# A two-product split matmul in one 512-column record: wide up projections and joined operands in a fused transformer kernel

## The reference, cut to what matters

```python
def sq_relu_mlp(h, w_in, w_out):            # both MLPs: 1024 -> 4096 -> 1024
    a = jax.nn.relu(h @ w_in)
    return (a * a) @ w_out

def conv_glu(h, w_up, conv_w, conv_b, w_down):   # 1024 -> 2 x 2816 -> 1024
    gate, val = jnp.split(h @ w_up, 2, axis=-1)
    gate = depthwise_conv(gate, conv_w, conv_b)  # three taps along the tokens
    return (jax.nn.silu(gate) * val) @ w_down
```

## Time and profile before

| | |
|---|---|
| median of 3 runs | 1146.64 us (1145.39 to 1147.46) |
| the profiled execution | 1149.56 us |
| its span in the trace | 1147.8 us |
| granted TensorE clock, mean | 0.968 |
| PE busy | 1036.6 us, 90% |
| DVE busy | 708.3 us, 62% |
| ACT busy | 551.6 us, 48% |

### The profile page before, as it was taken

The page is one execution under the profiler, slowest core; times in us unless marked ns, Lnnn a source line. Parts: engine busy times, 40 slices in busy tenths (PEclk is TensorE's granted clock), DMA queues, the critical chain, the costliest instruction groups (busy, mean ns, idle before and its releaser), DMA issues.

```text
span 1147.8 us, 15792 instructions
## 1 busy us (share of the span) xinstructions
PE 1036.6 (90%) x6172; PEld 897.9 (78%) x6172; DVE 708.3 (62%) x964; ACT 551.6 (48%) x746; POOL 97.3 (8%) x74
## 2 busy tenths in 40 slices
PE   3877899999999997889999999999789779999995
PEld 1655579888897876779999887989666568999994
DVE  5566655788766547466767664455477466666664
ACT  3464636676544556444545443542533235544442
POOL 0003000575300010000000000000000000000000
PEclk9897999999999999989999999999999889999998
DMA  4342436677753553455777642332200044544531
GB/s 170 103 123 107 129 111 237 252 275 261 293 183 110 183 183 110 147 184 210 278 293 276 224 186 74 111 124 97 97 15 0 1 165 148 205 178 176 208 128 55
DMA packets 28976, 183.92 MB, mean 160 GB/s; under 512 B 3456, under 2 KB 4992, under 8 KB 9344
## 3 DMA queue, kind: packets, MB, share of 16 engines
q1 hardware_dynamic: 23328, 153.69, 36.6%
q0 software_dynamic: 3456, 25.17, 6.1%
q10 hardware_dynamic: 2144, 4.42, 1.6%
HBM read 180.64 MB, written 2.62 MB: 160 GB/s over the span
## 4 chain that ended last, share of the span: by engine, by line
PE 54%; issue 20%; DVE 13%; ACT 7%; DMA 4%; POOL 1%; DVEq 0%; ACTq 0%; POOLq 0%; SPq 0%
PE bank L619 15%; PE bank L620 14%; PE bank L621 14%; DVE split L1656 4%; ACT split L1166 4%; PE bank L628 2%; DMA raw<-w_mlp 2%; PE bank L1075 1%; PE bank L1057 1%; PE bank L855 1%; DMA work<-in_ctx 1%; DVE acts L1824 1%; POOL stat L550 1%; ACT arena L1167 1%; DMA t5c<-in_t_cols 1%
## 5 line engine op out<-in xcount | busy, mean ns | idle before, releaser
L1656 DVE TENSOR_TENSOR split<-raw,split 128x2048 fp32r<-128x2048 f32 (+3 forms) x133 | 301.5, 2267 | 296.0 <-ACT split L1166 290.4
L1166 ACT ACTIVATE split<-raw 128x2048 fp32r<-128x2048 f32 (+3 forms) x133 | 247.5, 1862 | 307.3 <-PE bank L621 272.8
L619 PE MATMUL bank<-acts,split 128*128 128x256 f32 (+1 forms) x1024 | 290.6, 284 | 1.4 <-DVE split L1656 1.1
L620 PE MATMUL bank<-acts,split 128*128 128x256 f32 (+1 forms) x1024 | 289.7, 283 | 0.0
L621 PE MATMUL bank<-acts,split 128*128 128x256 f32 (+1 forms) x1024 | 289.6, 283 | 0.0
L619 PE MATMUL bank<-split,acts 128*128 128x512 f32 (+3 forms) x616 | 243.7, 396 | 32.8 <-DVE split L1656 9.7
L620 PE MATMUL bank<-split,acts 128*128 128x512 f32 (+3 forms) x616 | 238.9, 388 | 0.0
L621 PE MATMUL bank<-split,acts 128*128 128x512 f32 (+3 forms) x616 | 238.1, 386 | 0.0
L619 PEld LDWEIGHTS bank<-acts,split 128*128 128x128 f32 (+1 forms) x1024 | 194.8, 190 | 5.5 <-DVE split L1656 2.3
L620 PEld LDWEIGHTS bank<-acts,split 128*128 128x128 f32 (+1 forms) x1024 | 194.8, 190 | 2.2
L621 PEld LDWEIGHTS bank<-acts,split 128*128 128x128 f32 (+1 forms) x1024 | 194.7, 190 | 0.4
(11 more groups left out here) (233 smaller groups left out, 1113.5 us busy)
## 6 DMA issues: line engine op xcount, KB each, us to landing
raw<-w_mlp SPq DMA_DIRECT2D x64, 1024.0 KB, 4.9
raw<-w_glu SPq DMA_DIRECT2D x22, 1024.0 KB, 5.4
work<-w_ada POOLq DMA_DIRECT2D x12, 1024.0 KB, 5.1
raw<-w_qkv SPq DMA_DIRECT2D x12, 1024.0 KB, 4.8
bias<-w_ada POOLq DMA_DIRECT2D x12, 1024.0 KB, 5.1
arena<-w_glu_down SPq DMA_DIRECT2D x22, 512.0 KB, 3.3
raw<-w_mla_o SPq DMA_DIRECT2D x4, 1024.0 KB, 4.8
raw<-w_moba_o SPq DMA_DIRECT2D x4, 1024.0 KB, 4.8
```

Of the source, the lines that this page charges most:

```text
L619: pe.matmul(out_, a[0], b[0], start=first, stop=False)
L620: pe.matmul(out_, a[0], b[1], start=False, stop=False)
L1166: return act.activation(out_, in_, ACT.Copy)
L1656: v.tensor_tensor(split[:, c % 2, 1, 0:n], raw[:, c % 2, 0:n], split[:, c % 2, 0, 0:n].bitcast(F32), ALU.subtract).then_inc(lo_ready, 1)
```

## The change

A new record form, `wide_product`: the high part of the weights multiplies the high and the low part of the tokens in one 512-column matmul, the high part's result in columns 0 to 255 of a bank and the low part's in 256 to 511; the low part of the weights times the high part of the tokens is a 256-column matmul into columns 0 to 255. The two halves must be added by whoever empties the bank, and each 128 features take a whole bank, so an up step takes two banks.

- The first 14 of 16 up steps of each MLP (`WIDE = 14`) and all 22 of the GLU take this form: 32 records in place of 48. The last two of each MLP stay as they were.
- MLPs: DVE adds the halves with two `tensor_reduce` operations (`halves_added`) ahead of `split_lo` in its queue, into `relu_t`; ACT's relu then reads and writes `relu_t`.
- GLU: DVE adds the halves of gate and value with two `tensor_reduce` operations into `gsum`, first in its step; the middle tap waits for the first of them (`glu_gate`) and reads `gsum`, as do the outer taps and the product.
- dt, xs and B: `both_unit` has latents and context as the two halves of a 512-column moving operand, three records in place of six.

```diff
+            def wide_product(bank, w, f, k):
+                ws = tuple(p[:, k, f * P:(f + 1) * P] for p in w)
+                pe.matmul(bank[:, :].rearrange("p (a b) -> p a b", a=2), ws[0], acts[:, 0, :, k * T:(k + 1) * T],
+                          start=k == 0, stop=False)
+                return pe.matmul(bank[:, 0:T], ws[1], acts[:, 0, 0, k * T:(k + 1) * T], start=False, stop=k == KD - 1)
...
+                    elif s < WIDE:
+                        wide_unit(c0 + n, u0, s, i)
                     else:
-                        cols_unit(c0 + n, u0 + up_step(name, s), (0, 1), (0, 0), i)
+                        gemm_gone(pe, u0 + WIDE - 1)
+                        cols_unit(c0 + n, u0 + up_step(name, s), (0, 1), (0, 0))
...
+            def both_unit(c, u, f):
+                w = slot(c, KD, 256)
+                gemm_start(u)
+                for k in range(KD):
+                    ins = product(gbank(u)[:, :].rearrange("p (a b) -> p a b", a=2),
+                                  tuple(p[:, k, f * P:(f + 1) * P] for p in w), both_pair(k), k == 0, k == KD - 1)
+                ins.then_inc(gemm_ready, 1)
...
                 for f in range(2):
-                    cols_unit(GC["xs"] + j, GU["xs"] + 2 * j + f, (f, f), (0, 1))
+                    both_unit(GC["xs"] + j, GU["xs"] + 2 * j + f, f)
...
-                act.activation(gact[:, b, :], gbank(u)[:, 0:T], ACT.Identity, scale=w, bias=bb).then_inc(glu_mid, 1)
+                act.wait_ge(glu_gate, 4 * k + (s + 1))
+                act.activation(gact[:, b, :], gsum[:, b, 0:T], ACT.Identity, scale=w, bias=bb).then_inc(glu_mid, 1)
...
+                    for f, bank in enumerate(wide_banks(GU[name], s)):
+                        ins = v.tensor_reduce(relu_t[:, s % 2, f * T:(f + 1) * T],
+                                              bank[:, :].rearrange("p (a b) -> p b a", a=2), AX.X, ALU.add)
...
                 def chunk(n, i=None):
+                    if not seq[n][0] and seq[n][1] < WIDE:
+                        halves_added(seq[n][1], i)
                     used(c0 + n, i, 8)
...
+                gemm_out(v, u, i)
+                for f, bank in enumerate(wide_banks(GU["glu"], s)):
+                    v.tensor_reduce(gsum[:, b, f * T:(f + 1) * T], bank[:, :].rearrange("p (a b) -> p b a", a=2), AX.X,
+                                    ALU.add).then_inc(gemm_free[u % 4] if f else glu_gate, 1)
                 v.wait_ge(glu_mid, 4 * k + (s + 1))
```

More of the change, by code:

```diff
@@ L148 @@
 HID0 = dict(mlp0=0, mlp1=16, glu=32)
+WIDE = 14
+RELU0 = dict(mlp0=0, mlp1=WIDE)
 RAW = ("m0", "h1", "m1")
@@ L300, in program @@
         prod_t = view(arena, 2048, 2, T)
+        gsum = view(arena, 2560, 2, 2 * T)
         final = arena[:, 8192:8192 + D]
@@ L702, in cols_unit, with wide_start, wide_unit, first_wide @@
                 ins.then_inc(gemm_ready, 1)
+            def wide_start(u0, s, i=None):
+                if s < 2:
+                    gemm_start(u0 + 2 * s)
+                    gemm_start(u0 + 2 * s + 1)
+                else:
+                    u = u0 + s - 2
+                    pe.wait_ge(gemm_free[u % 4], u // 4 + 1 if i is None else i + (u // 4 + 1))
+            def wide_product(bank, w, f, k):
[3 more added lines that the diff above has]
+                return pe.matmul(bank[:, 0:T], ws[1], acts[:, 0, 0, k * T:(k + 1) * T], start=False, stop=k == KD - 1)
+            def wide_unit(c, u0, s, i=None):
+                w = slot(c, KD, 256)
+                wide_start(u0, s, i)
+                for f, bank in enumerate(wide_banks(u0, s)):
+                    for k in range(KD):
+                        ins = wide_product(bank, w, f, k)
+                ins.then_inc(gemm_ready, 1)
+            def first_wide(c, u0, name, tiles=4, units=2):
+                w = slot(c, KD, 256)
+                wide_start(u0, 0)
+                for k0 in range(0, KD, tiles):
+                    pe.wait_ge(act_lo, LO[name] - 4 + units * (k0 // tiles + 1))
+                    for f, bank in enumerate(wide_banks(u0, 0)):
+                        for k in range(k0, k0 + tiles):
+                            ins = wide_product(bank, w, f, k)
+                ins.then_inc(gemm_ready, 1)
             def first_up(c, u, name, tiles=4, units=2):
@@ L894, in modulation_and_context @@
                     pe.wait_ge(normed, 4)
+                    gemm_gone(pe, GU["mlp1"] + WIDE - 1)
                     for m in range(4):
@@ L926, in _, with both_pair @@
             values(1, 0)
+            def both_pair(k):
+                return tuple(acts[:, :, p, k * T:(k + 1) * T] for p in range(2))
+            def both_unit(c, u, f):
+                w = slot(c, KD, 256)
+                gemm_start(u)
+                for k in range(KD):
+                    ins = product(gbank(u)[:, :].rearrange("p (a b) -> p a b", a=2),
+                                  tuple(p[:, k, f * P:(f + 1) * P] for p in w), both_pair(k), k == 0, k == KD - 1)
+                ins.then_inc(gemm_ready, 1)
             both = rows_of(0) + rows_of(1)
@@ L932, in _ @@
             w = slot(c, KD, 16)
[L933 to L936, removed]
+            for k in range(KD):
+                ins = product(gbank(u)[0:16, :].rearrange("p (a b) -> p a b", a=2), tuple(p[:, k, :] for p in w),
+                              both_pair(k), k == 0, k == KD - 1)
             ins.then_inc(gemm_ready, 1)
```

47 lines of the change are left out of this document (33 added, 14 removed).

## The result

The changed kernel took 1152.72 us (median of 6 runs, 1151.77 to 1158.68) against 1146.76 for the kernel before (6 runs, 1145.39 to 1150.11): ratio 1.0063, 95% interval 1.0041 to 1.0086, some 6 us slower. The forecast was 1144.9 and its range ended at 1151.5. The profiled execution took 1151.77 us, span 1149.9, so in the traces only 2.1 of the 6 us are to be seen. The rest is looked for in the granted clocks of all runs, at the end of the part on the prediction.

A forecast was written before the change was run, and what follows sets the result against it. PE was taken to bound the joined stage, the GLU's steps and most of `mlp1`, with splits or ACT/DVE chains elsewhere. Joined −2.2, `mlp0` −2.0, `mlp1` −1.3 and GLU +3.8 gave −1.7 on 1146.64: 1144.9 us, range 1139.5 to 1151.5.

The forecast's parts named there:

- What bounds the kernel: PE sets the pace in some stretches, splits or ACT/DVE chains in others; the GLU chain's 0.33 us slack decides.
- The cost of a record: Each PE record has a fixed cost of 0.0133 us, so wide pairs save 0.21 us per up step.
- Rival (b): Two-piece operands pay the fixed cost twice, so PE gains nothing: total +7.4, 1154.0 us; chance 0.10.
- Joined: In dt, xs and B, 56 tiles save 0.040 us each, all of it passing: −2.2 us.
- `mlp0`: Shorter ups in the first MLP, about half hidden between down 3 and down 10: −2.0 us.
- Rival (c): Reductions are slow, by their own rate or beside POOL in `mlp0`: total +4 to +8, around 1152; chance 0.12.
- `mlp1`: In the second MLP, +1.3 before the first down, then twelve wide steps at PE's pace, −2.56: sum −1.3 us.
- The +1.3: At `mlp1`'s start two reductions stand before `split_lo`, so the first down comes 1.3 us later against its up.
- The reduction's price: One DVE reduction of 512 PSUM elements to 256 results takes 0.69 us, between bounds of 0.42 and 1.23.
- The GLU's period: Chain of 8.89 against PE's 8.29 makes a steady GLU step 8.59 us, +0.085; +1.5 over 18 periods.
- Rival (a): The chain stays hidden in the GLU and PE's 8.29 rules: total −7.2, 1139.4 us; chance 0.12.
- The clock: Longer waits at the GLU's first and last down cost +1.8 and +0.7 us; no term for slower records after them.

The follow-up runs named there:

- grouped: The changed kernel with each wide unit's 512-column records run first, then its 256-column ones, instead of alternating: 1148.91 us, ratio 1.0023 to the kernel before.
- joined: The kernel before with only the joined dt, xs and B units added: 1144.61 us, ratio 0.9980.
- glu_only: The kernel before with only the wide GLU added: 1155.68 us, ratio 1.0075.
- before_reorder: The kernel before, with the GLU's down chunk split ahead of the product's split on ACT and DVE: 1147.25 us, ratio 0.9997.
- after_reorder: The changed kernel, with the GLU's down chunk split ahead of the product's split on ACT and DVE: 1146.03 us, ratio 0.9991 to the kernel before.
- filler: The changed kernel plus unread 512-column matmuls, nine before the GLU's first down and twelve before its last: 1150.18 us, ratio 1.0027 to the kernel before.
- mlps: The kernel before with only the wide MLPs added: 1146.02 us, ratio 0.9995.
- mlps_joined: The kernel before with the wide MLPs and joined units, its GLU left as it was: 1145.03 us, ratio 0.9998.

## Why the prediction was wrong, point by point

**What bounds the kernel: right.** The GLU's slack of 0.33 us decided its period, and the kinds of stretch behaved as described. Two steps failed: the price of a wide pair, and, what put the time outside the range, a PE wait priced without the slower records behind it.

**The cost of a record: the saving of a wide pair came to half, and this is the first step that failed.** 0.0133 us per record is indeed a cost of the record at one width; joined units saved 0.038 per tile (forecast 0.040; only dt gave 0.06 us in place of 0.32), and so did grouped pairs (0.193 of 0.21 per step). But the sum "one wide and one narrow 0.3464" took prices from runs of one width and put them into an alternating sequence. There a pair is mostly 0.353: of 0.21 us per up step 0.11 is left. Rival (b) blamed the two-piece operand; grouped has the same operand without the cost, and the joined units too, so (b) falls as a mechanism though its direction was right. Its point of decision, "about 1.7 records' worth, 0.009 us of 0.0133 lost", was loosely worked: what is lost, 0.0066 per pair, is half of a record's cost, and the GLU had already turned.

**Joined: right**, −1.9 for −2.2. **`mlp0`:** −1.4 for −2.0, by the smaller saving. Rival (c), that reductions beside POOL are slow or go straight into the loaded part, did not come: down 3 to 10 became 1.0 us shorter, though 83.9 to 84.6 us in three traces with narrow MLPs and 83.5 to 84.2 in five with alternating wide ones leave little of that certain. With POOL at work from 226.79 to 233.57 the pair of reductions at 227.76 took 1.28 us, as everywhere, while `split_lo` behind it took 3.35 (2.29 elsewhere). This bears out the Trainium skill ("SBUF — State Buffer", section "Who interferes with whom"), by which `tensor_reduce` never contends with GpSimd on trn2.

**`mlp1`: right in the traced sum by luck.** The first down was to come 1.3 us later against its up, and between the two traces it came 0.36 later (16.20 us after up 0's first record, 15.84 before). The +1.3 was nevertheless right. In the traced execution of before, DVE stood 0.87 us for the context's rows from DRAM. Timeline, DVE of before, then DVE and PE of joined, whose MLPs are those of before:

```profile
500.09 1.23 DVE L1618 CUSTOM_DVE_ANT_0 work<-work 128x1024 f32<-128x1024 f32 x1 [0.87 <-DMA work<-in_ctx]
```
```profile
497.59 1.23 DVE L1630 CUSTOM_DVE_ANT_0 work<-work 128x1024 f32<-128x1024 f32 x1
...
505.35 0.77 PE L619 MATMUL bank<-split,acts 128*128 128x512 f32 x1 [3.00 <-DVE acts L2039]
```

None of the twelve other traces has that wait. In those with narrow MLPs (joined, glu_only, before_reorder) the down comes 15.0 us after the up, in those with wide ones 16.2: 1.2 later. So the earlier trace rows carried a wait of one execution. The twelve steps gave 12 x 0.113 = 1.36 in place of 2.56, by the price of a pair. Of the change there remains −0.2; the −1.3 of the two traces is that, 0.84 of DMA wait and some 0.3 of lower clock in before.

**The reduction's price: right.** Chosen 0.69 between 0.42 and 1.23; groups by form, DVE of the kernel after:
```profile
L2523 DVE TENSOR_REDUCE arena<-bank 128x256 f32<-128x512 f32 x44 | 28.3, 686 | 6.0 <-PE bank L726 5.6
```
0.686 us; the chain grew to 8.85 (forecast 8.89), and the first down came 1.8 later, as forecast.

**The GLU's period: structure right, one term mis-sized and one missing.** 8.680 for 8.59, because PE's part was 8.51 for 8.29: 0.11 from the widths and 0.11 from the slow first record of a down that came late. Half of 0.22 enters the period, 0.11, of which 0.02 is made good by the chain: 0.09 a step and 1.7 us in eighteen. That ACT and DVE rule and not PE alone, after_reorder shows. Rival (a), that the chain stays hidden, fell.

**The clock: the step that put the time outside the range.** The prediction priced waits in us of waiting and left PE's records after a wait at the upper clock, a term at nothing without a reason. In the trace the two longer waits brought 1.4 and 1.6 us of slower records, and filler took both away; with it the kernel is at 1150.18 us, inside the range. The rows had the sign: PE's first record after the 3.83 us at `mlp1`'s start lasts 0.77 us, after the 2.60 at the last down 0.47, and in all thirteen traces that first down of `mlp1` runs partly at the lower level.

**From the traces to the median.** Between the profiled executions only +2.1 us; between medians +6.0. The difference of the stages as traced is −4.7 + 8.8 = +4.1; the profiled execution of before also lost 1.6 between the MLPs by chance, so +2.5 (its last record is 2.53 later). In the stages are also the 1.1 us of chance at `mlp1` (above). Without them, and without the lower clock at the GLU's two ends, the change is worth −3.5 + 5.8 = +2.3, where the forecast had −1.7.

To compare the medians take each run's mean granted clock c and span: 2 x (1 − c) x span is the time at 1.2 GHz. Mean over the timed runs: after 83.3 us; before 71.5, from the 64 runs beside the experiments on its parts, since the clocks of before's six runs beside after are not on record. If PE worked in all of that time, half of it would be loss: (83.3 − 71.5)/2 = 5.9 us, and 2.3 + 5.9 = 8.2, where the mean spans differ by 6.8. The same sum for the kernels of the first experiments, with the mean difference of spans in brackets: glu_only 5.7 + 3.0 = 8.7 (7.9), filler 2.2 + 1.5 = 3.7 (3.3), grouped 0.6 + 0.9 = 1.5 (1.5), mlps −1.6 + 0.8 = −0.8 (−0.8), joined −1.9 − 0.9 = −2.8 (−3.0), mlps_joined −3.4 + 3.0 = −0.4 (−1.2), after_reorder −4.9 + 4.8 = −0.1 (−1.6), before_reorder −0.7 + 1.0 = 0.3 (−0.1). It closes within 1.5 us and is too high where the lower level lasts longest, which would follow if PE waits in part of it. This is an account and no experiment: shown by an intervention is the lower clock at the GLU's two ends, 3.1 us in the traces. The rest of the kernel after's extra time at 1.2 GHz, and why mlps_joined and after_reorder spend 6 to 10 us more there than before, stay open.

## What to carry to other kernels

Merging matmuls to save a fixed cost per record pays only where PE sets the pace. Group the records by width instead of alternating them, which here turned a saving of 0.11 us per step into 0.19. Before adding an operation to the chain that empties a bank, work out the chain's slack over a whole period, and the round of each engine in it, and look for work in it that need not wait (here two splits, swapped at no cost, made a loss of 6 us a gain of 7 together with the grouping). And price a longer PE wait not by its length alone: look at the granted clock in the records after it. Compare a row on which a forecast rests with more than one execution where there are any: a DMA wait of 0.87 us stood in one of thirteen here.

## What the runs showed of the hardware, unexpected

- fp32r records of 512 and 256 columns in turn: 0.353 us a pair; eight and eight: 0.3475; from runs of one width: 0.3464. Some alternating units, begun after a pause of PE, ran at 0.3464 all the same.
- After PE has waited for a down, the first record occupies 0.34 us instead of 0.23 (1024.12 to 1024.46), also at the upper clock.
- A record with a moving operand in two pieces of 256 columns takes 0.2271 us, with a plain one 0.2266.
- PE waits of 3.43 us were followed by records at 1.2 GHz in three traces of three, of 2.80 in three of four, of 2.60 to 2.69 in three of seven, of 1.7 and less at the same places in none.
- The kernel before itself ran between 1140.84 and 1151.58 us; its profiled span of 1147.8 has clock 0.968, and the best span here, 1139.1 of joined, 0.973. A thousandth of mean clock is some 1.1 us where PE sets the pace, so an edit of 2 us can be settled by stages in the trace but hardly by the total.
